# Moving 24 gathered-row columns from the gate and output-projection stages to the recurrent stage of a hybrid decoder step

## What is computed

```
x -> x + Merge(DiffAttn(n), RGLRU(n)),  n = RMSNorm(x)
x -> x + PEER(RMSNorm(x));   final RMSNorm

proj = n @ w_in                       # q | k | v | lru input | ga | gl
lru:   causal conv, r, i = sigmoid(xb @ lru_wa), sigmoid(xb @ lru_wx)
       h_t = a_t * h_(t-1) + u_t      # per channel, along the tokens
merge: (sigmoid(ga) * (att @ w_att_up) + sigmoid(gl) * (lru @ w_lru_up)) @ w_out
PEER:  each token picks 8 x 16 = 128 of 16384 experts
       act = gelu(dot(peer_u[eid], x)),  out = sum(gate * act * peer_v[eid])
```

## Time and profile before

| what | value |
| --- | --- |
| median of three runs | 4226.32 us |
| the profiled execution, its own time | 4220.9 us |
| its span, first to last instruction | 4219.1 us |
| mean granted TensorE clock | 0.869 |
| TensorE busy | 3375.1 us, 80% of the span |
| VectorE busy | 2659.8 us, 63% |
| GpSimd busy | 1483.0 us, 35% |
| ScalarE busy | 603.6 us, 14% |
| mean DMA rate | 312 GB/s |

### The profile page before, as it was taken

How to read it: one execution, slowest core, us unless ns; L and a number is a source line. 1 busy time by engine, 2 the same in 40 slices (tenths; PEclk the granted TensorE clock), 3 DMA queues, 4 the chain that set the end, 5 groups by cost and what they waited for, 6 DMA issues and landing times. The chain is left out here.

```text
span 4219.1 us, 33125 instructions
## 1 busy us (share of the span) xinstructions
PE 3375.1 (80%) x12703; PEld 2273.1 (54%) x12703; DVE 2659.8 (63%) x3901; ACT 603.6 (14%) x1485; POOL 1483.0 (35%) x868
## 2 busy tenths in 40 slices
PE   7979999959856888889998694122899996899990
PEld 6858888847644333367776573112644446544430
DVE  2350000676987666564556689999777679856668
ACT  2430000101222211200000101222300004200010
POOL 0000000013533656433445435886233322322236
PEclk9989999989978888899999897555699995699995
DMA  5424444457966999999989877998499998899999
GB/s 164 136 90 153 147 160 143 133 204 278 402 269 245 424 423 424 395 337 339 354 328 368 333 296 295 410 419 338 189 421 420 423 374 285 308 424 423 424 423 371
DMA packets 367904, 1317.40 MB, mean 312 GB/s; under 512 B 19541, under 2 KB 237302, under 8 KB 238594
## 3 DMA queue, kind: packets, MB, share of 16 engines
q0 software_dynamic: 124416, 939.58, 54.8%
q1 hardware_dynamic: 242542, 375.35, 25.1%
q10 hardware_dynamic: 788, 0.36, 0.0%
HBM read 1308.38 MB, written 6.83 MB: 312 GB/s over the span
## 5 line engine op out<-in xcount | busy, mean ns | idle before, releaser
L231 POOL DMA_INDIRECT area<-in_peer_u_dram,area x544 | 941.9, 1731 | 1994.6 <-POOLq L1328 907.7
L242 DVE CUSTOM_DVE_ANT_0 area<-area 128x2048 f32<-128x2048 f32 x544 | 1230.7, 2289 | 276.7 <-DMA area<-in_peer_u_dram,area 274.8
L1719 PE MATMUL PS<-area 128*128 128x512 f32 x2048 | 879.3, 592 | 0.0
L248 DVE SCALAR_TENSOR_TENSOR area<-area 128x2048 f32<-128x2048 f32 x288 | 677.0, 2351 | 194.2 <-DMA area<-in_peer_v_dram,area 168.1
L231 POOL DMA_INDIRECT area<-in_peer_v_dram,area x288 | 483.1, 1678 | 686.5 <-DVE area L248 595.6
L1719 PEld LDWEIGHTS PS<-area 128*128 128x128 f32 x2048 | 389.1, 190 | 489.8 <-issue 489.8
L1705 PE MATMUL PS<-area 128*128 128x64 f32 x1024 | 243.0, 425 | 333.5 <-issue 233.0
L1133 PE MATMUL PS<-area 128*128 128x256 f32 (+1 forms) x2048 | 474.4, 394 | 16.3 <-DMA area<-in_w_in_dram 11.3
L1133 PEld LDWEIGHTS PS<-area 128*128 128x128 f32 x2048 | 390.2, 191 | 98.3 <-DMA area<-in_w_in_dram 11.8
L1705 PEld LDWEIGHTS PS<-area 128*128 128x128 f32 x1024 | 225.7, 329 | 351.8 <-issue 261.4
L1182 DVE TENSOR_TENSOR area<-area,PS 128x256 f32<-128x256 f32 (+1 forms) x32 | 14.0, 438 | 457.7 <-PE PS L1143 457.7
(11 more groups left out here) (296 smaller groups left out, 2605.7 us busy)
## 6 DMA issues: line engine op xcount, KB each, us to landing
area<-in_peer_v_dram SPq DMA_DIRECT2D x128, 1024.0 KB, 9.1
area<-in_w_in_dram SPq DMA_DIRECT2D x56, 2048.0 KB, 8.2
area<-in_w_out_dram SPq DMA_DIRECT2D x16, 2048.0 KB, 9.0
area<-in_peer_wq_dram SPq DMA_DIRECT2D x16, 2048.0 KB, 9.5
area<-in_w_att_up_dram SPq DMA_DIRECT2D x16, 1024.0 KB, 5.7
area<-in_w_lru_up_dram SPq DMA_DIRECT2D x16, 1024.0 KB, 8.2
area<-in_peer_u_dram,area POOLq DMA_INDIRECT x544, 11.0
area<-in_x_prompt_dram SPq DMA_DIRECT2D x8, 1024.0 KB, 7.1
```

Of the source, the lines that this page charges most:

```text
L231: g_.indirect_dma_start(ring[SLOT[c]], None, io[("peer_u", "peer_v")[table]][0], bass.IndirectOffsetOnAxis(ap=slot_col(eid0, eid1, tb, j), ...
L242: v.tensor_tensor_reduce(row, row, Xn[(0, 1, 0, 0, 1)[tb]], 1.0, 0.0, ALU.mult, ALU.add, act).then_inc(s_used, 1)
L248: v.scalar_tensor_tensor(dst, row, act, dst, ALU.mult, ALU.add).then_inc(s_used, 1)
L1719: ins = pe.matmul(PS[:, 4 * b + q, :], spread[i // 32][:, i % 32, P * b:P * (b + 1)], vrows[n % 3][:, 512 * q:512 * (q + 1)], start=False, ...
```

## The change

Three numbers of the table change: in trunk 1 VectorE takes 11 columns instead of 8 after each of the eight convolutions of stage 1, 8 instead of 10 at each of the eight chunks of stage 5, and 5 instead of 6 at each of the eight chunks of stage 6. That is +24, -16 and -8. After stage 6 the same columns have been taken as before.

```diff
         for g in range(2):
-            stage1(g, [6] + [8] * 8 if g else None)
+            stage1(g, [6] + [11] * 8 if g else None)
             stage2(g, 4 if g else 0)
             stage3(g, 1 if g else 0)
             if g:
                 stage4(22, 8)
-            stage5(g, 10 if g else 0)
-            stage6(g, 6 if g else 0)
+            stage5(g, 8 if g else 0)
+            stage6(g, 5 if g else 0)
             stage7(g, 8 if g else 0)
```

## The result

The changed kernel takes 4269.3 us, the median of four runs from 4256.18 to 4270.32 us, against 4225.98 us before (four runs). The medians are 43 us apart. The ratio on record is 1.0094 with a 95% interval of 1.0079 to 1.0109, so slower, by 33 to 46 us. The forecast was 4270 us.

A forecast was written before the change was run, and what follows sets the result against it. The prediction took VectorE's chain to bound stage 1 and TensorE stages 5 and 6, apart from two weight stalls. Stage 1 pays 55 us, stages 5 and 6 return 6 and 5: +44 us on 4226.3, 4270 us, range 4252 to 4290 us.

The forecast's parts named there:

- the two weight stalls: TensorE waits for weights: chunk 1 of stage 5 takes 14.3 us more than its successors, stage 6 waits 14.53 us.
- VectorE's chain bounds stage 1, TensorE stages 5 and 6: Trunk 1: added columns cost VectorE 2.213 us each in stage 1; fewer columns win only within 28.8 us of stalls later.
- The floor of 50.8 us in stage 1: Least that stage 1 pays: 53.1 us of added columns less the 2.3 us wait for first gates they fill.
- Row waits in stage 1: DMA engines slower than VectorE by 0.7 us in six weight-loading blocks of stage 1: 4 us, making 55 us in all.
- the upper bound from the earlier trace: Most that stage 1 pays: three columns a block at 2.92 us, over eight blocks less 2.3 us, 67.8 us.
- What stage 5 gives back: Stall of chunk 1 shrinks as two to four fewer columns precede the weight landing: 6 us, ends 2 and 14.3.
- my own price: DMA time of one column of 1.049 MB at 419 GB/s: 2.50 us.
- What stage 6 gives back: Weight load for chunk 2 lands among 15 instead of 18 columns: 5 us, ends 2 and 14.5.
- Sum: Whole kernel: + 55 - 6 - 5 = +44 us, against the median 4270 us.
- late weights: Rival, stage 1: weight landings above 45 us make VectorE wait for gates, +55 us, 4281 us; chance 0.10.
- Both stalls vanish at the floor price: Rival: stages 5 and 6 lose all 28.8 us of stalls, stage 1 pays 50.8, +22 us, 4248 us; chance 0.06.
- Faster, because the DMA engines pace stages 5 and 6: Rival: every removed column gives 2.50 us, 60 us against 50.8 paid, -9 us, 4217 us; chance 0.02.

The follow-up runs named there:

- half_w: Changed kernel, but six weight loads in stage 1 of trunk 1 bring half their rows (1 MB instead of 2): 4261.1 us, 1.0085 against the kernel before.
- front7: Kernel before, with only 7 columns moved to stage 1, from the first two chunks of stage 5 and first three of stage 6: 4219.4 us, ratio 0.9990.
- reverse: Kernel before with columns moved the other way, 7 a block in stage 1, 11 a chunk in stage 5, 6 in stage 6: 4211.0 us, ratio 0.9960.
- s1_11_s5_7: Kernel before with 11 columns a block in stage 1, all 24 taken from stage 5 (7 a chunk), stage 6 at 6: 4274.2 us, ratio 1.0108.

## Why the prediction was right

The sign and the mechanism came as forecast: VectorE's chain through stage 1 pays, with rows late beside the weights, and the two weight stalls give a part back. That the number agrees to a microsecond (4270 against 4269.3 us) is luck: two terms were each 7 to 8 us off, and their errors cancelled.

- **VectorE's chain bounds stage 1, TensorE stages 5 and 6.** Shown by the chunks of 46.56 us that stayed with 8, 10 and 11 columns, and by the blocks that followed the number of columns: where no row wait stands they last 22.0, 24.1, 26.3, 28.5 and 32.9 us at 6, 7, 8, 9 and 11 columns.
- **The floor of 50.8 us in stage 1.** 53.1 us of columns less 2.3 us, and the wait is gone as said. ScalarE's second wait gave 0.9 us more (4.7 to 3.8 us).
- **Row waits in stage 1: this term was mis-sized.** I took 4 us; it measured 11.3 us more than before in the first profile, 12.6 us in the second, and stage 1 paid 62.4 and 63.9 us instead of 55. "Near the 1.04 that such blocks show now" treated a block as a sum of DMA work. The sum holds on average (1.03 in a 36.6 us block), but the rows are late at the end of a run of columns, not on average: the ring holds six and the run is eleven, so the seventh column of a block can be fetched only when its first has been used. In the five blocks that wait (first profile) the eighth, ninth or tenth column is the first to do so (0.2 to 2.0 us), and the next follow some 2.9 us apart. That makes 10.3 us more in the longest block, over the 8.76 us a block of the upper bound from the earlier trace rows; the total stays under its 67.8 us because the bound counts eight blocks and only five are hit (the 4 us counted six). The bound had the right picture of the spacing. The half_w run shows, and the last two blocks agree, that the weight loads make the difference. (50.8 us and 11.3 us less ScalarE's 0.9 us are 61.2 us; the last 1.2 us are open.)
- **What stage 5 gives back: also mis-sized,** 14.3 us instead of 6. I counted the fetches ahead of the landing and took a little more than two. If all four missing columns of chunks 0 and 1 counted, that is 10 us by my own price, as `front7` supports, which took out just these four and gave 10.3 us; with the wait went 2.1 us in which the first 64 matmuls after it had run slower (17.80 us against 15.68 us for the 64 ahead of it, with a granted clock of 0.92 over that chunk and 1.00 over each of the next) and 0.45 us for the up-projection's weights. The 4 us that `front7` lacks vary or hang on chunk 2; which is open.
- **What stage 6 gives back.** 5 us forecast, 6.3 us measured, and 1.9 us more in stage 7, which I had not counted.
- **Sum.** 55 - 6 - 5 = 44 forecast; 62.4 - 14.3 - 6.3 - 1.9 = 39.9 in the first profile, 41.9 in the second, 43 in the medians.

The rivals: *late weights* did not happen. The landing went to 32.9 us, far from 45, and VectorE never waited for gates. What I had not seen is that TensorE would be held by ScalarE, which kept it from running ahead; it decided nothing. *Both stalls vanish at the floor price* was half true, one stall vanished, but not the floor. *Faster, because the DMA engines pace stages 5 and 6* is excluded for stage 5 by `reverse`, where 11 columns left the chunks at 46.56 us, and by s1_11_s5_7, where 7 did, and for stage 6 by its last six chunks, 128.4 us with six columns and 128.6 us with five; for stage 5 it becomes true at 12.

## What to carry to other kernels

A column beside an engine that is not the bound is free only up to the point where the DMA engines it shares run full (here 11 columns a chunk of stage 5, not 12), and a stall that a late transfer makes hangs on what is in flight just before it: 7 columns ahead of the two stalls gave 16.7 us of what 24 gave, 22.5 us. Before moving such work to another stage, look for a wait on the same engine at the head of the same stage: starting three columns some 29 us earlier removed a 14 us stall at no price. And a share of busy DMA time (1.04 and 1.03 here) did not say how late the last rows of a run are (0.4 and 11.7 us in all); for that the ring's depth is held against the run's length.

## What the hardware showed beyond expectation

A weight load of 2 MB lands after 30.7 us beside the gathers of 8 columns a block and after 32.9 us beside 11 (medians of four), though the engines need some 6.6 us for it, the prediction's estimate from the earlier trace rows. Rows beside such a load came 2.9 us apart, in stage 5 before the change and in stage 1 after it, against the 2.50 us that 419 GB/s make (and 2.48 to 2.50 us in two blocks of `half_w`). The stall of stage 6 was 14.5 to 19.8 us in five profiles with the same 18 columns ahead of its load; the five differ in what stages 1 and 5 take, and what moves the stall by these few microseconds is open.
